# A modulation vector summed on VectorE between the steps of a recurrence instead of in the scan stages, with earlier loads put off, four tiles at once on TensorE, and a reordered tail

## The chip, the cores and the metric

One core of a Trainium2 chip runs one kernel: a whole transformer-like layer in float32. The metric is the device time of one execution in microseconds (us), the median of the runs of one kernel. The core has a matrix engine (TensorE, "PE" in the profile, its weight loads "PEld"), VectorE ("DVE"), ScalarE ("ACT"), GpSimd ("POOL") and SyncE ("SP"), which here only issues DMAs. SP, ACT and POOL each have a DMA queue of their own; all share 16 DMA engines.

## The reference, cut to what matters

The layer has a modulation (adaLN), a mixer with two branches, and a PEER feed-forward with 512 expert rows for each of the 256 tokens.

```python
mod_l = split(silu(c) @ w_ada + b_ada, 6)             # 2048 x 12288: six vectors of 2048
n = modulate(rmsnorm(h), mod[0], mod[1])              # for the 256 tokens x and the 256 of ctx
z = n @ w_in                                          # 2048 x 7168
ya = s5_mixer(z[:, :1024])                            # state-space scan, 64 groups of 16 channels
yb = lru_mixer(z[:, 1024:2048]) * gelu(z[:, 2048:3072])   # conv, gates, gated linear recurrence
m = sigmoid(z[:, 3072:5120]) * (ya @ w_proj_a) + sigmoid(z[:, 5120:]) * (yb @ w_proj_b)
h = x + mod[2] * (m @ w_out)
f = modulate(rmsnorm(h), mod[3], mod[4])
q = f @ w_query; top 16 of 16384 experts for each token and head (8 heads)
out = rmsnorm(h + mod[5] * sum_k g_k * gelu(f . u[e_k]) * v[e_k])    # rows of 2048 gathered
```

Modulation vector 3 (`LATE_CHUNKS[1]`, the shift of the second norm) is the one that moves here: silu(c) times 16 row blocks of 128 x 2048 of `w_ada`, 1 MB each.

## The kernel before, in words

The program is a queue written out by hand for each engine, with semaphores between them. Weights come in units of 1 MB through a ring of five slots (`w_ring`). A planner (`plan`) writes the list `units` with slot and freeing semaphore; SP issues the loads in that order, and each waits until its slot is free (`load_unit`), so that a load that waits holds up all behind it.

1. Front (0 to 173 us). x and ctx are transposed; for g = 0 to 7 four units of `w_ada` are multiplied for two blocks of the first two vectors (`group_unit`, L1223), ScalarE moves them (`group_rows`), VectorE scales nT, and `front_product` (L1248) adds this part of the first six columns of z. The weights of `front_product` are `w6[g]`, 768 KB each, loaded from ACT's queue four groups ahead (`load_w6`); POOL loads the S5 matrices (`cnat`, 1 MB) after three units are used. `output_weights` transposes them in g = 1 and 2.
2. Recurrence (173 to 348 us). Ten more columns of z, 512 wide (`columns`, L1261), nearly one for each k = 0 to 7 of the recurrence: TensorE gates(k), ScalarE `gates`, `roots`, VectorE `conv`, `q_of`, `scans` (rt, ig and ag have three buffers). Sixteen units of vector 2 (`late_unit`, L1204) are multiplied on TensorE, two in a row in the middle of each column, through slots 3 and 4. ScalarE does in order for each column: evacuate it, gates(k), roots(k-1). POOL stores u (`u_dram`) for each k and waits for it.
3. `lag_zero` (L1276, 256 small matmul records) with the weights Bb that VectorE has just made (L1049 to L1054), then eight G columns, 256 wide.
4. Sixteen scan stages. In each: TensorE does two columns of z for the gates (32 records each), the matmuls of `s5_params` (L1372, L1382), `s5_states` (L1395), `s5_out` (L1410, L1412). ScalarE evacuates; POOL does `imaginary_product`, `rotations`, two stores and `build_pb`; VectorE does `state_scan`, `build_m` and `last_vector` (L1134): one unit of vector 3, in three pieces. Each stage loads three units: two of w_in, one of w_ada.
5. `last_rows(1)` sums vector 3 over the partitions, then projections with w_glu, w_pa, w_pb (to 893 us) and w_out (to 1007 us), with vectors 4 and 5 on VectorE.
6. PEER (from 1009 us): 256 gathers of u rows and 256 of v rows, 1 MB each, from POOL's queue, v four behind u (`LAG`); VectorE does the dots (L1881), in groups of two (`GROUP`) ScalarE the gelu and the diagonal weights, TensorE adds the v rows (L2016). The weights of a group are made after the dots of the next group. At the end the final norm.

Of the kernel before, what the change touches and what calls it, by code (L numbers as in the profile page):

```python
# [9 lines left out]
ALU = mybir.AluOpType  # L10
# [3 lines left out]
P = 128  # L14
# [23 lines left out]
LATE_PER_PAIR = {3: 0, 4: 4, 5: 4, 6: 4, 7: 4}  # L38
# [15 lines left out]
def build(nc, t):  # L54

    ctx = ExitStack()
    with ctx:
# [90 lines left out]
        for n, count in LATE_PER_PAIR.items():  # L148
            plan_first(n + 1, turn[(2 * n + 2) % 3])
            plan_late(count)  # L150
            plan_second(n + 1, turn[(2 * n + 3) % 3])
        last_wide = n + 1
# [6 lines left out]
        last_at = []  # L159
# [52 lines left out]
        def unit(pe, u):  # L212
# [6 lines left out]
              (ada_at, last_at, pair_at, glu_at, fin_at, fin_count), acc_full, acc_free, unit_done, ada_used,  # L219
# [33 lines left out]
def mixer(nc, t, ctx, sem, w_ring, ident, mT, nT, scol, notfirst, units, load_unit, unit, places, acc_full, acc_free,  # L253
          unit_done, ada_used, late_sems, fin_full, fin_used, mods_dram, u_dram, y_dram, gates_dram):

    ada_at, last_at, pair_at, glu_at, fin_at, fin_count = places
    last_used, last_sum, mod_free, mods_out, vec_in = late_sems
    with ExitStack() as st:  # L258
# [19 lines left out]
        last_c = sb("last_c", [P, 256])  # L278
# [28 lines left out]
        def take(n):  # L307
# [15 lines left out]
        kst = take(GS * NLAG * H).rearrange("p (g n h) -> p g n h", g=GS, n=NLAG)  # L323
# [12 lines left out]
        sums = [(zu.rearrange("p b s c -> p (b s c)"), 0, 1024), (big[:, 13888:14656], 1024, 1792),  # L336
                (last_c[:, :], 1792, 2048)]
# [21 lines left out]
        id0, id_ready = sem("id0"), sem("id_ready")  # L359
# [10 lines left out]
        bb_ready, kz_full, kz_done = sem("bb_ready"), sem("kz_full"), sem("kz_done")  # L370
        gst_out, sgate_in = [sem("gst_out0"), sem("gst_out1")], [sem("sgate_in0"), sem("sgate_in1")]
# [39 lines left out]
        def toeplitz(sp, s):  # L411

            sp.wait_ge(k_copied, 3 * s + 3)
# [8 lines left out]
        def _(sp):  # L422
# [14 lines left out]
            for u in range(RING, NUNITS_HERE + RING):  # L437
                s, x = divmod(u - STAGE_UNITS, 3)
# [5 lines left out]
        def _(pool):  # L444
            link = stepper(pool, pool_s)

            pool.memset(ident[:], 0.0).then_inc(id0, 1)
            pool.wait_ge(id0, 1)
# [10 lines left out]
            pool.wait_ge(ada_used, 3)  # L459
# [16 lines left out]

            pool.wait_ge(acc_free, V0 + NB)
# [13 lines left out]

            for k in range(KW):
                pool.wait_ge(acc_free, U0 + k + 1)
# [110 lines left out]
        def _(act):  # L604
# [39 lines left out]
            for g in range(NG8):  # L644
# [5 lines left out]
                if g == 0:  # L650
# [1394 lines left out]
```

## Time and profile before

| | |
|---|---|
| median of 3 runs | 2380.9 us (2379.0 to 2382.27) |
| the profiled execution | 2378.94 us; span from first to last instruction 2377.1 us |
| busy | PE 2025.9 us (85%), DVE 1393.9 (59%), POOL 1041.7 (44%), ACT 457.7 (19%) |
| front | 0 to 172.8 us |
| recurrence | 172.8 to 348.05 us |
| lag_zero | 348.05 to 360.37 us |
| G columns and first column of stage 0 | 360.37 to 424.82 us |
| scan stages, from one L1372 to the last L1418 | 424.82 to 737.37 us |
| projections | 737.37 to 1007 us |
| PEER | 1009 to 2377.1 us |

The span is what one execution shows; some 2 us of the measured time lie around it. In a row of the timeline the first number is the start, the second the time to the end of the last of its instructions, and the bracket is the idle time of that engine ahead of it with what ended it. A float32 matmul is two records (x32 is 16 matmuls).

### The profile page before, as it was taken

To read this page: it belongs to the slowest core of one execution; us is meant where nothing else is said; L and a number is where in the kernel's file an instruction comes from. 1 tells how busy PE (TensorE), PEld (TensorE's weight loads), DVE (VectorE), ACT (ScalarE), POOL (GpSimd) and SP (SyncE) were. 2 spreads that over 40 slices of the span, in tenths; PEclk is the share of its full clock that TensorE was granted. 3 is DMA by queue.
4 is the path that set the end of the run, shared out by engine and by line. 5 is a ranking of instruction groups with operands and counts; after the bars stand their busy time and mean duration, and the time that the engine had idled before them with its cause. 6 is when DMAs were issued, how large, how long until landed. Compare 5 with 4: busy or idle time off the path is not lost.

```text
span 2377.1 us, 21789 instructions
## 1 busy us (share of the span) xinstructions
PE 2025.9 (85%) x8106; PEld 1176.7 (50%) x8106; DVE 1393.9 (59%) x2142; ACT 457.7 (19%) x977; POOL 1041.7 (44%) x883
## 2 busy tenths in 40 slices
PE   5999999999999999989789888777777777777776
PEld 3443348887887878875344444222322222222222
DVE  4643651799995533546555664565566566655644
ACT  3116740233331000121011111101110111111011
POOL 1001005799993100035455555555555455555552
PEclk8999999999999999999999999999999999999999
DMA  9965558565657898879999999999999999999996
GB/s 335 305 195 146 208 179 159 182 192 172 200 188 237 302 335 303 294 274 411 413 414 418 421 421 422 421 422 421 421 421 422 422 421 422 421 422 422 421 422 255
DMA packets 253017, 789.33 MB, mean 332 GB/s; under 512 B 25160, under 2 KB 170768, under 8 KB 177520
## 3 DMA queue, kind: packets, MB, share of 16 engines
q0 software_dynamic: 80528, 558.18, 58.0%
q1 hardware_dynamic: 160704, 220.31, 28.0%
q10 hardware_dynamic: 11680, 9.44, 1.3%
q8 instruction: 65, 1.06, 0.2%
q14 instruction: 40, 0.33, 0.0%
HBM read 774.20 MB, written 9.47 MB: 330 GB/s over the span
## 4 chain that ended last, share of the span: by engine, by line
DMA 39%; PE 20%; issue 1%; POOL 1%; DVE 0%; ACT 0%; DVEq 0%; ACTq 0%; POOLq 0%
DMA vb<-in_peer_v,eidx 39%; PE ps L2016 11%; PE ps L1917 4%; PE ps L1972 3%; PE ps L1949 1%; POOL vb L1613 0%; DMA w_ring<-in_w_out 0%; PE ps L1936 0%; POOL nT L1613 0%; DVE h L1855 0%; DVE f L1854 0%; PE ps L1987 0%; DVE h L1862 0%; ACT L1688 0%; ACT L1719 0%
## 5 line engine op out<-in xcount | busy, mean ns | idle before, releaser
L2016 PE MATMUL ps<-vb,diag 128*128 128x512 f32 x2048 | 954.1, 613 | 274.0 <-DMA vb<-in_peer_v,eidx 269.7
L2016 PEld LDWEIGHTS ps<-vb,diag 128*128 128x128 f32 x2048 | 378.5, 193 | 839.9 <-DMA vb<-in_peer_v,eidx 439.3
L1613 POOL DMA_INDIRECT vb<-in_peer_v,eidx x256 | 422.3, 1650 | 547.7 <-PE ps L2016 536.7
L1881 DVE CUSTOM_DVE_ANT_0 nT<-nT,f 128x2048 f32<-128x2048 f32 x170 | 389.3, 2292 | 340.1 <-DMA nT<-in_peer_u,eidx 339.4
L1261 PE MATMUL ps<-nT,w_ring 128*128 128x256 f32 (+1 forms) x1600 | 427.5, 426 | 0.3 <-issue 0.3
L1261 PEld LDWEIGHTS ps<-nT,w_ring 128*128 128x128 f32 x1600 | 303.0, 192 | 114.8 <-issue 82.3
L1881 DVE CUSTOM_DVE_ANT_0 mT<-mT,f 128x2048 f32<-128x2048 f32 x86 | 197.0, 2291 | 188.2 <-DMA mT<-in_peer_u,eidx 188.0
L1719 ACT ACTIVATE gel<-hd 128x2 f32<-128x2 f32 x128 | 26.0, 204 | 1118.2 <-DVE hd L1881 1118.2
L1613 POOL DMA_INDIRECT nT<-in_peer_u,eidx x170 | 174.2, 1025 | 51.8 <-issue 51.8
L1917 PE MATMUL ps<-w_ring,mT 128*128 128x256 f32 x512 | 111.5, 380 | 4.4 <-PEq L258 2.3
L1613 POOL DMA_INDIRECT mT<-in_peer_u,eidx x86 | 88.4, 1028 | 47.0 <-issue 25.9
L1917 PEld LDWEIGHTS ps<-w_ring,mT 128*128 128x128 f32 x512 | 96.9, 190 | 19.1 <-issue 6.1
L1972 PE MATMUL ps<-fT,w_ring 128*128 128x256 f32 x448 | 98.9, 379 | 0.6 <-ACT scol L1647 0.6
L1972 PEld LDWEIGHTS ps<-fT,w_ring 128*128 128x128 f32 x448 | 84.9, 190 | 16.4 <-issue 5.5
L1446 PE MATMUL ps<-big,w_ring 128*128 128x256 f32 x384 | 85.5, 384 | 5.0 <-DMA w_ring<-in_w_proj_a 3.5
L1703 ACT ACTIVATE diag<-ident,wgt 128x128 f32<-128x128 f32 x256 | 88.5, 393 | 2.2 <-DVE wgt L1839 0.3
L1446 PEld LDWEIGHTS ps<-big,w_ring 128*128 128x128 f32 x384 | 73.7, 193 | 17.1 <-issue 4.8
L1248 PE MATMUL ps<-nT,big 128*128 128x512 f32 x144 | 67.8, 606 | 2.6 <-ACT nT L648 2.6
L494 POOL DMA_DIRECT2D u_dram<-zu x8 | 4.4, 547 | 144.7 <-ACT zu L715 144.7
L1604 POOL DMA_DIRECT2D mods_dram<-diag x1 | 0.6, 600 | 121.1 <-DVE diag L1867 121.1
L470 POOL DMA_DIRECT2D mT<-in_lru_w_r x4 | 2.7, 687 | 116.0 <-PE ps L1223 116.0
L594 POOL DMA_DIRECT2D big<-gates_dram x16 | 11.4, 717 | 93.2 <-DVE mT L1176 93.2
(367 smaller groups left out, 2108.1 us busy)
## 6 DMA issues: line engine op xcount, KB each, us to landing
w_ring<-in_w_ada SPq DMA_DIRECT2D x96, 1024.0 KB, 7.0
w_ring<-in_w_in SPq DMA_DIRECT2D x50, 1024.0 KB, 5.3
w_ring<-in_w_out SPq DMA_DIRECT2D x16, 1024.0 KB, 7.4
w_ring<-in_peer_w_query SPq DMA_DIRECT2D x16, 1024.0 KB, 25.5
w_ring<-in_w_proj_b SPq DMA_DIRECT2D x8, 1024.0 KB, 7.9
w_ring<-in_w_proj_a SPq DMA_DIRECT2D x8, 1024.0 KB, 7.8
big<-in_w_in ACTq DMA_DIRECT2D x6, 768.0 KB, 7.9
big<-big SPq DMA_DIRECT2D x128, 32.0 KB, 3.5
```

The costliest lines, as they stand in the source:

```text
L594: pool.dma_start(sgate[:, c % 2, x].rearrange("p (k n) -> p k n", k=2), gates_dram[x * KD + 2 * c:x * KD + 2 * c + 2].rearrange("k p n -> ...
L1248: last = pe.matmul(ps[:, acc_bank(b), :], w6[g][:, kb, b * P:(b + 1) * P], nT[:, k, :], start=(k == 0), stop=(k == KD - 1))
L1261: last = pe.matmul(ps[:, (a + j) % 2, 0:hi - lo], w[k // UK][:, k % UK, j * P:(j + 1) * P], nT[:, k, lo:hi], start=(k == 0), stop=(k == KD ...
L1446: last = pe.matmul(ps[:, bank, j * T:(j + 1) * T], w[:, k, j * P:(j + 1) * P], y[:, k], start=(k == 0), stop=(k == KW - 1))
L1613: pool.indirect_dma_start(ring[m % n], None, table, bass.IndirectOffsetOnAxis(ap=eidx[:, i % 3, j:j + 1], axis=0))\
L1703: act.activation(diag[:, m % NDIAG], ident[:], ACT.Copy, scale=wgt[:, i % 2, m % K:m % K + 1])\
L1719: act.activation(gel[:, i % 2, lo:lo + GROUP], hd[:, i % 2, lo:lo + GROUP], ACT.Gelu_apprx_tanh)\
L1881: v.tensor_tensor_reduce(ub[m % n_u], ub[m % n_u], f[:, i // HEADS], 1.0, 0.0, ALU.mult, ALU.add, hd[:, i % 2, m % K:m % K + 1]).then_inc( ...
L1917: last = pe.matmul(ps[:, 4 * (c % 2) + i, 0:COLS], mT[:, k, i * P:(i + 1) * P], w[k // UK][:, k % UK, :], start=(k == 0), stop=(k == KD - 1))
L1949: last = pe.matmul(ps[:, 4 + i, j * P:(j + 1) * P], w[k // UK][:, k % UK, j * P:(j + 1) * P], fT[:, k, i * P:(i + 1) * P], start=(k == 0), ...
L1972: last = pe.matmul(ps[:, 4 + c % 2, j * T:(j + 1) * T], w[k // UK][:, k % UK, j * P:(j + 1) * P], fT[:, k, :], start=(k == 0), stop=(k == ...
L2016: last = pe.matmul(ps[:, 4 * tile + c, :], diag[:, m % NDIAG], vb[m % NV][:, c * 512:(c + 1) * 512], start=(r == 0), stop=(r == HEADS * K ...
```

## The change

- Vector 3 leaves the scan stages. `load_row` on POOL's queue brings its 16 blocks one by one into slot 4, each only after the block ahead of it is used (`last_used`); `row_vector` on VectorE adds them up (704 + 1344 columns): block 0 after the first four convs, block 2k+1 between `q_of(k)` and `scans(k)`, block 2k+2 between `scans(k)` and the next conv. POOL's loads stand ahead of the stores of u in its queue. `last_rows(1)` comes ahead of the scan stages, into bank 7. A stage then loads two units, not three.
- Vector 2's units go through slot 3 alone, one at the middle and one at the end of a column's half instead of two at the middle.
- `load_w6(g + 2)` after group g+1's rows, where it was `load_w6(g + 4)`; `cnat` waits for nine units, not three; `output_weights` in g = 3 and 4.
- VectorE makes Bb in the G columns (`input_weights` after k = 2 and 3), and `lag_zero` comes after the G columns.
- The kernel matmuls of `s5_params` (L1372) put group g's result at partition 32 g, all four groups of one r after another; ScalarE evacuates them with four activations of 16 x 224 where it had two of 16 x 448 (`k_copied` 5 for each stage, not 3).
- PEER: the last two groups of two become four of one, v rows close up from four to one behind u over the last six rows, and ScalarE does a square root on a dummy ahead of both norms.

```diff
-LATE_PER_PAIR = {3: 0, 4: 4, 5: 4, 6: 4, 7: 4}
+LATE_PER_PAIR = {3: (1, 0), 4: (3, 1), 5: (3, 1), 6: (3, 1), 7: (3, 0)}
...
-                ada_at.append(plan_ada(*late[n_late[0]], 3 + n_late[0] % 2))
+                ada_at.append(plan_ada(*late[n_late[0]], 3))
...
+        row_free = freed_by[4]
+        freed_by[4] = (last_used, KD)
...
-            if n >= len(pairs) - NSTAGE:
-                plan_last()
...
-        sums = [(zu.rearrange("p b s c -> p (b s c)"), 0, 1024), (big[:, 13888:14656], 1024, 1792),
-                (last_c[:, :], 1792, 2048)]
+        sums = [(last_c[:, :], 0, 704), (big[:, 13312:14656], 704, 2048)]
...
-            pool.wait_ge(ada_used, 3)
+            pool.wait_ge(ada_used, 9)
...
+            def load_row(k):
+                if k == 0:
+                    pool.wait_ge(row_free[0], row_free[1])
+                else:
+                    pool.wait_ge(last_used, k)
+                at = LATE_CHUNKS[1] * D
+                pool.dma_start(row_view(w_ring[:, 4]), t["w_ada"][0, k * P:(k + 1) * P, at:at + D])\
+                    .then_inc(row_in, 16)
+            load_row(0)
...
+            load_row(1)
             for k in range(KW):
+                for n in (2 * k + 2, 2 * k + 3):
+                    if n < KD:
+                        load_row(n)
                 pool.wait_ge(acc_free, U0 + k + 1)
                 pool.dma_start(u_dram[k], zu[:, k % 2]).then_inc(u_out, 16)
                 pool.wait_ge(u_out, 16 * (k + 1))
...
-                    load_w6(2)
-                    load_w6(3)
-                if g + 4 == NG8 - 1:
-                    act.wait_ge(s5_setup, 8)
-                if g + 4 < NG8:
-                    load_w6(g + 4)
...
+                if g + 2 < NG8:
+                    load_w6(g + 2)
...
-                for x in range(2):
-                    act.activation(kst[0:H, :, Q * x:Q * x + Q - 1, :],
-                                   ps[0:H, 2 + x, 0:GS * (Q - 1) * H].rearrange("p (g n h) -> p g n h", g=GS, h=H),
+                lags = kst.rearrange("p g (x n) h -> p g x (n h)", x=2)
+                for g in range(GS):
+                    act.activation(lags[0:H, g, :, 0:(Q - 1) * H], ps[32 * g:32 * g + H, 2:4, 0:(Q - 1) * H],
                                    ACT.Copy).then_inc(k_copied, 1)
...
             for k in range(4):
                 conv(k)
+            row_vector(0)
             for k in range(KW):
                 q_of(k)
+                row_vector(2 * k + 1)
                 scans(k)
+                if k < KW - 1:
+                    row_vector(2 * k + 2)
                 if k + 4 < KW:
                     conv(k + 4)
...
-                if s < NSTAGE:
-                    last_vector(s)
...
-                spots = ((), ()) if c < KW // 2 else ((7, 7), (7, 7))
+                spots = ((), ()) if c < KW // 2 else ((7, 15), (7, 15))
...
-            lag_zero()
             for c in range(KW // 2):
                 for _ in columns(G0 + 2 * c, T, 2 * T):
                     pass
+            lag_zero()
+            last_rows(1)
...
-                for g in range(GS):
-                    for r in range(2):
+                for r in range(2):
+                    for g in range(GS):
                         for x, part in ((1, slice(0, N)), (0, slice(N, P))):
-                            last = pe.matmul(ps[0:H, 2 + x, g * nk:(g + 1) * nk], Bb[part, r, s * GS + g, :],
+                            last = pe.matmul(ps[32 * g:32 * g + H, 2 + x, 0:nk], Bb[part, r, s * GS + g, :],
...
+    groups = [range(m, m + GROUP) for m in range(0, NI * K - 2 * GROUP, GROUP)]
+    groups += [range(m, m + 1) for m in range(NI * K - 2 * GROUP, NI * K)]
+    rows_behind = {m: LAG - 1 - (m - (NI * K - 3 * GROUP)) // GROUP for m in range(NI * K - 3 * GROUP, NI * K)}
...
+            act.activation(root_in, ident[:, 0:1], ACT.Sqrt)
             last_squares()
```

## Rows read from the trace of the kernel before

**Rows 1.** The page's chain that ended last, shares of the span by engine.
```profile
DMA 39%; PE 20%; issue 1%; POOL 1%; DVE 0%; ACT 0%; DVEq 0%; ACTq 0%; POOLq 0%
```

**Rows 2.** Windows: start:end, length, busy of five engines, PE clock, DMA share, GB/s.
```profile
0.00:45.00 45.00, 26.66 (x194) 17.38 (x194) 20.87 (x70) 18.15 (x28) 7.25 (x15) 0.92 1.01 324
...
172.80:348.05 175.25, 171.95 (x514) 67.86 (x512) 93.35 (x135) 111.62 (x154) 11.49 (x13) 1.00 0.50 167
348.05:360.37 12.32, 6.97 (x257) 6.75 (x256) 5.67 (x6) 1.88 (x2) 4.34 (x8) 0.85 0.96 293
...
424.82:737.37 312.55, 304.80 (x2265) 263.96 (x2265) 291.89 (x286) 106.93 (x198) 278.94 (x254) 0.99 0.61 187
644.68:725.05 80.37, 77.55 (x581) 67.00 (x581) 78.03 (x77) 28.53 (x52) 74.88 (x69) 1.00 0.61 190
```

**Rows 3.** Timeline of PE in the front.
```profile
41.52 3.70 PE L1248 MATMUL ps<-nT,mT 128*128 128x512 f32 x8
...
55.15 1.93 PE L1223 MATMUL ps<-w_ring,scol 128*32 128x256 f32 x16 [8.05 <-DMA w_ring<-in_w_ada]
57.01 5.04 PE L1248 MATMUL ps<-nT,mT 128*128 128x512 f32 x8
```

**Rows 4.** Timeline of PE: a late unit, and the start of lag_zero.
```profile
213.47 1.07 PE L1204 MATMUL ps<-w_ring,scol 128*32 128x512 f32 x8 [0.57 <-DMA w_ring<-in_w_ada]
...
351.32 6.28 PE L1276 MATMUL ps<-Cc,Bb 128*16 128x16 f32 x236 [3.19 <-DVE Bb L1054]
```

**Rows 5.** Timelines of ACT and DVE: roots(1), the first instruction of scans(1) and of scans(5).
```profile
234.36 1.15 ACT L698 ACTIVATE big<-big 128x512 f32<-128x512 f32 x2
...
235.61 0.69 DVE L1029 TENSOR_TENSOR big<-big 128x512 f32<-128x512 f32 x1 [6.42 <-ACT big L698]
...
309.93 0.69 DVE L1029 TENSOR_TENSOR big<-big 128x512 f32<-128x512 f32 x1 [10.35 <-ACT big L698]
```

**Rows 6.** DMA issues from 200 to 345 us: count, KB each, median us to landing.
```profile
w_ring<-in_w_ada SPq DMA_DIRECT2D x16, 1024.0 KB, 7.8
w_ring<-in_w_in SPq DMA_DIRECT2D x8, 1024.0 KB, 5.1
u_dram<-zu POOLq DMA_DIRECT2D x7, 256.0 KB, 4.0
```

**Rows 7.** Line L599, three POOL loads of 1 MB at 824 to 845 us.
```profile
DMA to landing us min/median/max: 7.9/10.7/11.8
```

**Rows 8.** Groups by form: count, busy us, mean ns of one, idle before.
```profile
L248 DVE SCALAR_TENSOR_TENSOR big<-w_ring,scol,big 128x2048 f32<-128x2048 f32 x15 | 35.2, 2344 | 0.3
...
L1134 DVE SCALAR_TENSOR_TENSOR zu<-w_ring,scol,zu 128x1024 f32<-128x1024 f32 x15 | 25.7, 1711 | 0.5
...
L1134 DVE SCALAR_TENSOR_TENSOR big<-w_ring,scol,big 128x768 f32<-128x768 f32 x15 | 20.2, 1347 | 0.5
...
L1134 DVE SCALAR_TENSOR_TENSOR last_c<-w_ring,scol,last_c 128x256 f32<-128x256 f32 x15 | 12.1, 806 | 0.5
```

**Rows 9.** Timeline of PE from one stage to the next.
```profile
606.03 1.71 PE L1372 MATMUL ps<-big,Bb 64*16 64x112 f32 x32
...
608.60 7.07 PE L1261 MATMUL ps<-nT,w_ring 128*128 128x256 f32 x32
...
615.85 0.62 PE L1412 MATMUL ps<-big 128*32 128x128 f32 x16
...
625.35 1.71 PE L1372 MATMUL ps<-big,Bb 64*16 64x112 f32 x32
```

**Rows 10.** The window of POOL's first round of stage work.
```profile
388.59:404.57 15.98, 15.68 (x73) 13.52 (x72) 4.12 (x4) 1.13 (x3) 14.94 (x17) 1.00 0.74 237
```

**Rows 11.** Timeline of the end: the last dot, the last v rows, the root.
```profile
2346.12 2.29 DVE L1881 CUSTOM_DVE_ANT_0 nT<-nT,f 128x2048 f32<-128x2048 f32 x1 [2.63 <-DMA nT<-in_peer_u,eidx]
...
2348.61 17.43 PE L2016 MATMUL ps<-vb,diag 128*128 128x512 f32 x40 [1.21 <-DMA vb<-in_peer_v,eidx]
...
2369.67 1.28 ACT L1688 ACT_TABLE_LOAD   x1
```

More of the change, by code:

```diff
@@ L1059, in late_rows, with lag_zero @@
+            def lag_zero():
+                step(tt(kzero[:], ident[0:H, 0:H].unsqueeze(1).to_broadcast([H, G, H]),
+                        dT[:].unsqueeze(2).to_broadcast([H, G, H]), ALU.mult))
+                for b in range(2):
+                    v.wait_ge(kz_full, b + 1)
+                    kz = kzero[:, b * 32:(b + 1) * 32, :].rearrange("p g h -> p (g h)")
+                    tt(kz, kz, ps[0:H, 4 + b, :], ALU.add).then_inc(kz_done, 1)
+                v.wait_ge(kz_done, 2)
             def late_rows(q):
@@ L1269, in columns, with last_rows @@
                     yield
+            def last_rows(q):
+                pe.wait_ge(last_used, KD * q)
+                if q == 2:
+                    pe.wait_ge(acc_free, L0 + KW)
+                for j in range(4):
+                    at = slice(j * 512, (j + 1) * 512)
+                    for total, lo, hi in (sums if q == 1 else [(fin_sum, 0, D)]):
+                        a, b = max(lo, at.start), min(hi, at.stop)
+                        if a < b:
+                            last = pe.matmul(ps[32 * j:32 * j + 32, (7, 0)[q - 1], a - at.start:b - at.start],
+                                             notfirst[:, 1:33], total[:, a - lo:b - lo], start=True, stop=True)
+                last.then_inc(last_sum, 1)
             def lag_zero():
@@ L1359, in _ @@
                     pass
+            lag_zero()
+            last_rows(1)
             def s5_params(s):
@@ L1469, in _ @@
                         fin(c, 1)
-                    last_rows(1)
                 if s < NSTAGE:
@@ L1616, in _ @@
             tu, tv = t["peer_u"][0], t["peer_v"][0]
-            for m in range(NI * K + LAG):
-                if m < NI * K:
-                    if m % K == 0:
-                        pool.wait_ge(idx_ready, m // K + 1)
-                    gather(m, tu, ub, u_in, u_used)
-                if m >= LAG:
-                    gather(m - LAG, tv, vb, v_in, v_used)
+            n_v = 0
+            for m in range(NI * K):
+                if m % K == 0:
+                    pool.wait_ge(idx_ready, m // K + 1)
+                gather(m, tu, ub, u_in, u_used)
+                while n_v <= m - rows_behind.get(m, LAG):
+                    gather(n_v, tv, vb, v_in, v_used)
+                    n_v += 1
+            for m in range(n_v, NI * K):
+                gather(m, tv, vb, v_in, v_used)
         @block.scalar
         def _(act):
+            act.activation(root_in, ident[:, 0:1], ACT.Sqrt)
             for c in range(NCH):
@@ L1877, in _ @@
                     v.wait_ge(gel_done, (i - 1) * (K // GROUP))
-                for m in range(GROUP * g, GROUP * (g + 1)):
+                for m in groups[g]:
                     n_u = len(ub)
```

151 lines of the change are left out of this document (71 added, 80 removed).

## The prediction

> **What bounds the kernel now.** I read the chain that ended last first: 39% of it is DMA of v rows and 20% TensorE [rows 1]. PEER is one DMA stream from 1070 us to the end, and the change leaves its 512 gathers alone. What comes before it shifts it as a whole, so a microsecond on TensorE before 1007 us is a microsecond of the kernel, as long as PEER's own start and end are counted apart.
>
> Then I cut the time before PEER into windows. In the recurrence TensorE works 171.95 of 175.25 us, around lag_zero 6.97 of 12.32, in the scan stages 304.80 of 312.55 [rows 2]. So TensorE is the bound nearly everywhere, and the reader should look for two things: waits between its instructions (the timeline of PE), and work of its own that gets shorter. But the scan stages are close to a second bound: VectorE is busy 291.89 us there and GpSimd 278.94 [rows 2]. From 644.68 to 725.05 us are four stages of 20.1 us, while a stage in which TensorE never waits takes 625.35 - 606.03 = 19.32 us [rows 2, 9]. VectorE and GpSimd stretch each other: a piece of 256 columns of `last_vector` takes 0.81 us and one of 1024 takes 1.71, where 2048 alone take 2.34 [rows 8].
>
> **Part by part.** *Front.* TensorE waits 8.05 us for a unit of w_ada, and its next eight records take 5.04 us where the same eight took 3.70 before the wait [rows 3]: 8.05 + 1.34 = 9.4 us. What is late is bytes: the queues bring 324 GB/s with the DMA engines full, 14.6 MB by 45 us [rows 2]. The unit waited for is the eighth. With x and ctx (4.2 MB), eight units (8.4) and two w6 (1.6), it needs 14.2 MB; three more w6 and cnat (3.4 MB) are in the same stream today and leave it. So it would be there at about 45 us, and TensorE comes for it at 46. I take all 9.4 us. Bounds: 6, if the stream, which then still owes cnat and one w6 per group, falls behind once more, and 10.3, if the group's own matmuls (1.93 us, also slow) get their speed back as well. That the later loads of w6 cost nothing rests on their cover: each has more than the time of one group to land.
>
> *Recurrence, TensorE's side.* The 16 late units stay. Four waits like the 0.57 us one [rows 4] make 3.3 us, being all that TensorE waits here (175.25 - 171.95) [rows 2]. With slot 3 alone, a unit needed at the end of a column can only be asked for when the one at the middle is used, some 7 us earlier (16 records, each twice as long as the 221 ns of the narrow columns [rows 9]), and a unit lands in 5.1 us when alone and 7.8 when others are in the queue [rows 6]. Eight such places with 0 to 1.1 us each: 0 to 8.8 instead of 3.3. I take no change, range -3.3 to +5.5.
>
> *Recurrence, VectorE's side.* This is where the change adds a wait. A column lasts (309.93 - 235.61) / 4 = 18.6 us, and VectorE waits 6.42 of them in front of `scans(1)`, 10.35 when no conv is left to do [rows 5]. Two blocks at 2.34 and a gap cost 4.9 us per k [rows 8]; this fits. But slot 4 is one buffer: block n+1 is asked for when block n is used, so a k cannot take less than 2 x 2.45 + 2L, L being the time from the use of a block to the landing of the next; scans, conv and q_of (12 us in two parts) lie beside the two loads. Behind the waiting block stand scans(k), the next conv and q_of, on which ScalarE's `roots` waits, and behind that its evacuation of the next column, for which TensorE waits two columns on. The last chance is column 15: its evacuation is needed when the first G column is done, 348.05 + 7.1 = 355.1 us. From scans(1) at 235.6: five turns of 4.9 + 2L to scans(6), then L + 2.45 for block 14, 2.5 for q_of(7), for which two passes over 1024 columns cost about one over 2048 [rows 8], 1.2 for the two roots [rows 5] and half of that for the evacuation, as wide as one root. 266.9 + 11 L = 355.1 gives L = 8.0. Up to there nothing shows; every microsecond above costs 11. No row shows such a load. From below: 256 KB from POOL's queue land in 4.0 us [rows 6], the other 0.79 MB take 2.3 us at the 324 GB/s of rows 2: 6.3. From above: 1 MB loads of POOL took 7.9 to 11.8 us, but with the DMA engines full [rows 7]. Here they are half full at 167 GB/s; 16.8 MB more make it 263 [rows 2]. So I take the lower end and 0.9 us of sharing, L = 7.2, cost 0.
>
> Beside it stands the Trainium skill, DMA: Bandwidth & Descriptors, Anatomy of one DMA: a GpSimd DMA takes 2.0 us + bytes / 436 GB/s by its fit, an estimate of 4.4 us for this load when alone, and L near that would make the cost 0 as well. The trace has no lone 1 MB load of POOL's queue to set beside the fit.
>
> *lag_zero.* TensorE waits 3.19 us for Bb in front of it, and of its 12.32 us it works 6.97 [rows 2, 4]. After the change Bb is made in the G columns, where VectorE has two short operations per column, and six more in two of the eight columns fit beside them. The 3.19 us go; of the other 2.2 idle us I credit 0.8. Sum 4.0, bounds 0 and 5.3. `last_rows(1)` leaves the end of the stages and comes in here at the same price: 0.
>
> *Scan stages.* Two effects. TensorE's own: L1372 takes 1.71 us for 32 records, today two tiles at a time [rows 9]; afterwards eight tiles are addressed in turn. L1412, four tiles with 128 columns, needs 0.62 us for 16 records [rows 9], 39 ns each; lag_zero's small ones need 27 ns each (6.28 us for 236) [rows 4]. 32 records make 1.24 or 0.85 us; the streams themselves would allow 0.43. I take 0.9, since 112 columns over eight tiles hide below the issue: 0.8 us less, 18.5 us a stage. The other: VectorE loses 1.71 + 1.35 + 0.81 = 3.9 us a stage [rows 8], so the stages of 20.1 us go. 16 x 18.5 = 296 for 312.55: 16.5 us. Bounds: 3.4 if the tiles give nothing (16 x 19.32 = 309.1) and 23.9 if they run freely (288.6). ScalarE's evacuation grows from two to four activations; it is busy 106.93 of the 312.55 us [rows 2] and hides them. SP's Toeplitz copies stand ahead of other units now, but two units a stage leave them early.
>
> A rule sets a floor under the tiles: by the Trainium skill, TensorEngine Tiling (Array Packing), Instruction Overhead, each matmul costs some 60 cycles whatever its size, an estimate of 25 ns at 2.4 GHz and of 0.8 us for 32 records. The 27 ns of lag_zero's records [rows 4] agree with it, and by it the free run to 288.6 us would be out of reach.
>
> *PEER.* The last u row lands at 2346.12, a v row at 2348.61, so a row takes 2.49 us; the four v rows still out are in at 2358.6, but TensorE works five rows at 3.49 until 2366.0 [rows 11]. Afterwards the order ends u255, v254, v255: u255 lands at 2353.6, its dot and weights are ready near 2357, and only two rows (7.0 us) are left: 2.5 us less. A table load of 1.28 us stands in front of the last root [rows 11], half of it beside VectorE's three small steps: 0.7 us, and much the same at the head of PEER: 1.3. Together 3.8, bounds 1 and 5.
>
> Sum: 9.4 + 0 + 4.0 + 16.5 + 3.8 = 33.7. Against the profiled execution: span 2377.1 - 33.7 = 2343.4, time 2378.9 - 33.7 = 2345.2. That execution is 2 us under the median; 2380.9 - 33.7 = 2347.2.
>
> **The rivals.** (1) *The blocks land late.* L of 9.5 instead of 7.2 costs 16.5 us in the recurrence: 2364. For it: the loads share the engines with late units in bursts; against it: the mean share stays below three quarters. Chance 0.13.
> (2) *The same, slower than before.* From L = 8.0 + 33.7 / 11 = 11.1 on the whole gain is gone. At the 11.8 us of rows 7 TensorE waits 42 us at the end of the recurrence: 2389. It needs engines as full as there; the window's 167 GB/s speak against it. Chance 0.05.
> (3) *The tiles do nothing* (one after another, or a switch between tile shapes that costs as much): stages of 19.32 us, 309.1, time 2360. Against it: L1412's 39 ns. Chance 0.10.
> (4) *GpSimd becomes the stages' bound.* Its first round, with VectorE busy for 1.13 us only, lasts 15.98 us with one small DMA issue in it [rows 10]; with a second and larger one some 16.8; in the late stages 20.1. VectorE's busy time falls by a fifth, so the 3.3 us of stretch by as much: 19.4 us a round. It starts with about 10 us in hand and would use up 14: 4 us more, 2351; without that reserve 14 more, 2361. Beside it stands the Trainium skill, GPSIMD Engine Reference, Specifications: GpSimd shares its SBUF interfaces with VectorE. Chance 0.10.
>
> **How the numbers follow.** The forecast has 0.62: 2347, its own range 2337 to 2356. The best bounds of all parts give 2336; the rivals that are still gains lie at 2351 to 2364. I give 2337 to 2367, which leaves out rival 2, a part of rival 1 and the far good end. A measurement of this kernel tells 0.2% (4.8 us) from no change. Faster: forecast, rivals 3 and 4 and nearly all of 1, 0.93; same 0.02; slower 0.05.
>
> **What would show it.** TensorE's first wait for w_ada near 55 us gone, and the windows' end of the front near 163 us; L1276 with no wait on Bb; L1372 at 0.9 us with its 32 records; stages of 18.5 us with VectorE idle 3 to 4 us in each; L2016's last unbroken run shorter than five rows. Wrong would be: VectorE waiting for w_ada by way of POOL's queue with the idle time in front of scans gone, and then TensorE waiting in front of a G column for ScalarE; or GpSimd without a pause and TensorE waiting in front of L1382 or L1410.

## The result, and the profile after

The changed kernel takes 2344.85 us in the median of 4 executions (2331.79 to 2350.51), the kernel before 2379.95 (4 executions): a ratio of 0.9844, 95% interval 0.9807 to 0.988. Forecast were 2347, range 2337 to 2367. The total is right, but two of its terms are not, and they cancel. The four executions also lie 19 us apart, where those of the kernel before lie within 4.4 us; the profiled one is the fastest (time 2331.79, span 2329.7). A second profile of the same kernel (`after_again` below, span 2340.8) is nearer the median, and each stretch is read in both.

| stretch, us | before | after | after again | change | forecast |
|---|---|---|---|---|---|
| front, to the first column | 173.18 | 162.17 | 163.02 | -11.0, -10.2 | -9.4 |
| recurrence, to the end of its last column or late unit | 174.87 | 172.81 | 173.74 | -2.1, -1.1 | 0 |
| G columns, lag_zero, column 1 of stage 0 | 76.77 | 73.16 | 81.34 | -3.6, +4.6 | -4.0 |
| stages, 15 periods | 300.23 | 272.05 | 272.05 | -28.2, -28.2 | -16.5 |
| last stage to the first v row | 344.04 | 343.28 | 344.91 | -0.8, +0.9 | 0 and head of PEER |
| first v row to the end | 1308.0 | 1306.2 | 1305.7 | -1.8, -2.3 | -3.8 with the head |

The windows of the profile after, which answer to [rows 2] (start:end, length, busy us of PE, PEld, DVE, ACT, POOL, PE clock, DMA share, GB/s), for the first 45 us, the recurrence, the stages, and four stages of them:

```profile
0.00:45.00 45.00, 26.70 (x194) 17.44 (x194) 20.86 (x70) 18.15 (x28) 3.72 (x11) 0.92 1.01 338
161.85:334.98 173.13, 172.51 (x514) 67.31 (x512) 125.42 (x158) 112.57 (x156) 20.00 (x28) 1.00 0.77 253
408.14:691.40 283.26, 283.26 (x2265) 243.31 (x2264) 225.02 (x237) 113.91 (x230) 259.20 (x254) 1.00 0.51 147
571.00:643.83 72.83, 72.83 (x589) 62.44 (x594) 59.39 (x65) 30.28 (x60) 67.33 (x66) 1.00 0.52 151
```

In the stages TensorE never waits any more: 283.26 us busy in 283.26. VectorE is idle (72.83 - 59.39) / 4 = 3.4 us in each. GpSimd has 67.33 busy us in the four, so it pauses for 1.4 us in each, and TensorE never waits for it.

The timeline of PE after, at the places of [rows 3], [rows 4] and [rows 9]:

```profile
45.18 1.93 PE L1245 MATMUL ps<-w_ring,scol 128*32 128x256 f32 x32
47.05 3.70 PE L1270 MATMUL ps<-nT,mT 128*128 128x512 f32 x8
...
336.32 41.68 PE L1283 MATMUL ps<-nT,w_ring 128*128 128x256 f32 x192 [1.34 <-issue]
379.69 14.05 PE L1283 MATMUL ps<-nT,w_ring 128*128 128x256 f32 x64 [1.69 <-issue]
393.67 6.54 PE L1313 MATMUL ps<-Cc,Bb 128*16 128x16 f32 x255
...
570.95 0.60 PE L1410 MATMUL ps<-big,Bb 64*16 64x112 f32 x32
571.48 1.09 PE L1420 MATMUL ps<-ident,big 128*128 128x128 f32 x8
...
589.16 0.60 PE L1410 MATMUL ps<-big,Bb 64*16 64x112 f32 x32
```

The wait of 8.05 us for w_ada is gone, the eight records behind it take 3.70 us again, lag_zero starts with no wait for Bb. L1410 (L1372 of before) ends its 32 records so early that the next line starts 571.48 - 570.95 = 0.53 us after it, and a stage takes 589.16 - 570.95 = 18.21 us. New are two waits of TensorE in the G columns, for nothing that the profile names. In `after_again` the second is 6.17 us:

```profile
338.76 27.86 PE L1283 MATMUL ps<-nT,w_ring 128*128 128x256 f32 x128 [2.00 <-issue]
372.80 30.89 PE L1283 MATMUL ps<-nT,w_ring 128*128 128x256 f32 x128 [6.17 <-issue]
```

The four columns behind it take 30.89 us where the four ahead took 27.86: from 369 to 379 us the granted clock is 0.50, the lower of the two levels (1.2 and 2.4 GHz). TensorE had stood since 366.6, and it worked from 372.80 on for 6 us at that clock. In the changed kernel's first profile the clock there is 1.00. The window of `after_again`:

```profile
369.00:379.00 10.00, 6.20 (x15) 4.99 (x16) 2.71 (x3) 0.00 (x0) 2.96 (x4) 0.50 1.09 231
```

The DMA side of it is the time from issue to landing of the w_in units that SP issues from 345 to 372 us, first in the profile after, then in `after_again`:

```profile
L211 SPq DMA_DIRECT2D w_ring<-in_w_in x4: 368/368/4436, 347.0 to 364.2; - x4
...
DMA to landing us min/median/max: 16.2/18.6/26.2
```

```profile
L211 SPq DMA_DIRECT2D w_ring<-in_w_in x4: 367/368/6922, 349.4 to 366.7; - x4
...
DMA to landing us min/median/max: 16.8/20.3/24.7
```

The unit issued at 349.4 in `after_again` lands 23.3 us later, at 372.7, and TensorE goes on at 372.80. The wait ahead of the first G column ends in the same way: its unit lands at 336.2 and 338.7 us in the two profiles, and TensorE starts at 336.32 and 338.76. What runs beside the units of the second wait are POOL's 32 loads of U (the copy of u that the scan stages read back from memory), 64 KB each; from 348 to 372 us the DMA engines are full and move 125 to 174 GB/s (in stretches of 6 us). The first row is the kernel before, the second the profile after:

```profile
356.57 17.77 POOL L499 DMA_DIRECT2D nT<-u_dram  x32 [6.73 <-DMA u_dram<-zu]
342.78 17.78 POOL L514 DMA_DIRECT2D nT<-u_dram  x32 [7.06 <-DMA u_dram<-zu]
```

The kernel before has the same slow loads. Its w_in units of 372.6 and 376.0 us take 17.4 and 17.0 us, and TensorE waits for the first of them, which lands at 390.0:

```profile
L210 SPq DMA_DIRECT2D w_ring<-in_w_in x2: 367/368/368, 372.6 to 376.0; - x2
...
DMA to landing us min/median/max: 17.0/17.2/17.4
...
390.12 34.77 PE L1261 MATMUL ps<-nT,w_ring 128*128 128x256 f32 x160 [0.30 <-issue]
```

By this trace lag_zero is why it waits for 0.30 us only: while TensorE waited for Bb and did lag_zero (348 to 360 us), three units asked for at 348.2 to 349.2 could land (by 364.4), so that four units, enough for four columns, were there or nearly so when the G columns began at 360.37.

The blocks of vector 3 (L484, 16 loads by POOL), first how long VectorE waits for them (22.3 us in 8 waits), then their time from issue to landing:

```profile
  DVE last_c L1058: 22.3, 8
...
DMA to landing us min/median/max: 5.2/5.7/10.7
```

And the tail, which answers to [rows 11]: the last u dot, the last two v rows, the table load now beside them, the root.

```profile
2309.15 2.29 DVE L1916 CUSTOM_DVE_ANT_0 nT<-nT,f 128x2048 f32<-128x2048 f32 x1 [4.96 <-DMA nT<-in_peer_u,eidx]
...
2312.16 7.10 PE L2051 MATMUL ps<-vb,diag 128*128 128x512 f32 x16 [0.77 <-ACT diag L1735]
2312.39 1.28 ACT L1761 ACT_TABLE_LOAD   x1
...
2323.49 0.20 ACT L1720 ACTIVATE rss<-rss 128x1 f32<-128x1 f32 x1 [0.61 <-DVE rss L1894]
```

### The profile page after: what moved, and what is told of

Its sections match the earlier page's. It is cut to its first block, busy times and chain, and to the rows that moved or that the text cites. A ratio compares the mean times of both kernels' runs of the same rounds, so it can differ in the third digit from the quotient of the medians.

```text
span 2329.7 us, 21810 instructions
## 1 busy us (share of the span) xinstructions
PE 1998.1 (86%) x8106; PEld 1152.6 (49%) x8106; DVE 1368.2 (59%) x2128; ACT 465.4 (20%) x1013; POOL 1031.9 (44%) x899
## 4 chain that ended last, share of the span: by engine, by line
DMA 39%; PE 21%; issue 1%; POOL 1%; DVE 1%; ACT 0%; DVEq 0%; POOLq 0%
DMA vb<-in_peer_v,eidx 37%; PE ps L2051 12%; PE ps L1952 5%; PE ps L2007 4%; DMA nT<-in_peer_u,eidx 2%; POOL vb L1641 1%; PE ps L1984 1%; DMA w_ring<-in_w_out 0%; PE ps L1971 0%; DVE nT L1916 0%; PE ps L2022 0%; POOL nT L1641 0%; DVE h L1890 0%; DVE f L1889 0%; DVE h L1897 0%
## 5 line engine op out<-in xcount | busy, mean ns | idle before, releaser
L1752 ACT ACTIVATE gel<-hd 128x2 f32<-128x2 f32 (+1 forms) x130 | 26.3, 203 | 1125.8 <-DVE hd L1916 1125.7
L1486 PEld LDWEIGHTS ps<-big,w_ring 128*128 128x128 f32 x384 | 73.8, 193 | 16.8 <-issue 4.1
L1130 DVE TENSOR_TENSOR big<-big 128x512 f32<-128x512 f32 x32 | 37.4, 1169 | 53.7 <-ACT big L763 53.1
L484 POOL DMA_DIRECT2D w_ring<-in_w_ada x16 | 8.5, 534 | 122.9 <-DVE big L1058 122.9
```

What stands on the lines that cost most here:

```text
L1130: ins = tt(x, Ssb, rot[:, s % 2, r:r + 1].to_broadcast([P, 2, GS, NC]), ALU.mult)
L1486: last = pe.matmul(ps[:, bank, j * T:(j + 1) * T], w[:, k, j * P:(j + 1) * P], y[:, k], start=(k == 0), stop=(k == KW - 1))
L1752: act.activation(gel[:, i % 2, lo:hi], hd[:, i % 2, lo:hi], ACT.Gelu_apprx_tanh)\
```

## The experiments

**The changed kernel again** (`after_again`), no edit.

> The changed kernel once more, unchanged, since its four executions lay between 2331.8 and 2350.5 us where the kernel before stays within 4.4 us. Theory 1 (the clock): an execution near 2345 has stretches before PEER in which TensorE's granted clock is lower than in the profiled one, and the waits are the same; its span is then some 12 us longer in those stretches alone. Theory 2 (the loads): the same clock, but waits of TensorE for w_ada, of VectorE for rows or of PEER for u and v that the profiled execution does not have. Expected time 2345, range 2332 to 2351.

2341.17 us (2335.12 to 2343.86), ratio 0.9823 (0.9804 to 0.9842). Theory 2 in the main: of the 11.1 us between the two profiles, 0.9 lie in the front, 1.6 in the recurrence with the wait behind it, 7.5 from the first G column to stage 0 (4.5 of longer waiting and 3.0 of columns at the lower clock behind it), none in the 15 periods, 1.6 behind them, and -0.5 in PEER. All eight executions of the changed kernel together have a median of 2342.2.

**The tiles taken back** (`no_tiles`).

```diff
-                for r in range(2):
-                    for g in range(GS):
+                for g in range(GS):
+                    for r in range(2):
...
-                            last = pe.matmul(ps[32 * g:32 * g + H, 2 + x, 0:nk], Bb[part, r, s * GS + g, :],
+                            last = pe.matmul(ps[0:H, 2 + x, g * nk:(g + 1) * nk], Bb[part, r, s * GS + g, :],
```

> The changed kernel with the tiles of the s5_params kernel matmuls and their evacuation as before (one column tile, two activations, k_copied 3 a stage). Theory 1 (TensorE bounds the stages once vector 3 has left them, and the tiles are worth what their line shows): the line's 32 records take 1.71 us again instead of 0.60, a stage 18.2 + 1.1 = 19.3 us, 15.6 stages 17 us, so 2345 + 17 = 2362. Theory 2 (the tiles were only filling idle time and the relief of VectorE gave the stages their gain): a stage stays near 18.2, time 2345 to 2348.

2361.23 us (2358.27 to 2370.24). Two neighbouring stages in its timeline of PE:

```profile
437.11 1.71 PE L1410 MATMUL ps<-big,Bb 64*16 64x112 f32 x32
...
456.43 0.75 PE L1410 MATMUL ps<-big,Bb 64*16 64x112 f32 x12
```

456.43 - 437.11 = 19.32 us a stage, with no wait: theory 1. (The second row is cut by the window.) Without vector 3 TensorE alone bounds the stages, and the 1.11 us of the line are 1.11 us of the stage.

**Only the order taken back** (`tiles_g_outer`): the two loops as in the diff above, the four places kept.

> The changed kernel with the same four column tiles, but the loop over groups outside the loop over re and im, as before the change: four records in a row go to one column tile, two to each row half. Theory 1 (what matters is that neighbouring matmuls lie in different column tiles): the line goes back towards 1.7 us, a stage to 19.3, time 2362. Theory 2 (the placement alone does it): 0.6 us, 18.2 us a stage, time 2345. Something between, some 1.1 us, would mean that both row halves and the column tiles share in it: 2353.

2342.03 us (2338.19 to 2348.68), the line at 0.64 us, a stage 18.25 us. The expectation of theory 1 fell: it is not the turn but the place. Why 32 records at one partition range take 1.71 us and at four 0.64 in either order is not settled.

**The tiles alone on the kernel before** (`tiles_alone`): vector 3 stays in the stages.

> The kernel before with the tiles and the four activations alone; vector 3 stays in the stages. Theory 1 (VectorE with vector 3 holds the stages at 20.0 us, TensorE is no longer their bound): TensorE's line is 1.1 us shorter and its waits 1.1 us longer, stages 19.7 to 20.0, time 2375 to 2380. Theory 2 (TensorE alone bounds the stages and the effects add up): 15.6 x 1.1 = 17 us less, 2363.

2373.69 us (2372.66 to 2379.35), ratio 0.9975 (0.996 to 0.9989). Four stages and the first row of two of them:

```profile
590.34:670.70 80.36, 73.12 (x580) 62.57 (x581) 78.02 (x77) 30.31 (x60) 75.01 (x69) 1.00 0.62 191
```

```profile
590.34 0.43 PE L1410 MATMUL ps<-big,nT 128*32 128x128 f32 x8 [1.81 <-issue]
...
610.43 0.43 PE L1410 MATMUL ps<-big,nT 128*32 128x128 f32 x8 [1.82 <-issue]
```

VectorE is busy 78.02 of 80.36 us and the stage takes 20.09 us, to the hundredth what four stages of before took [rows 2]; TensorE's gain has become a wait of 1.8 us. The 15 periods together got shorter by 4.7 us. In the mean of the last 14 periods, 20.14 us before, the tiles alone save 0.25 us, vector 3's leaving alone 0.82, both together 1.93.

The mean hides how the periods of the kernel before differ: nine take 19.3 us (the first of them 18.3), four 20.1, one 21.15 and one 25.89. In the last TensorE waits, for nothing that the profile names, and then works at a granted clock of 0.61 (573.6 to 580.4 us), so that 32 records take 9.30 us and not 7.07:

```profile
573.64 0.42 PE L1410 MATMUL ps<-big,nT 128*32 128x128 f32 x8 [3.17 <-issue]
...
577.48 9.30 PE L1261 MATMUL ps<-nT,w_ring 128*128 128x256 f32 x32
```

So the 28.2 us of the 15 periods are 16.7 of the shorter line (15 x 1.11), 8.4 of these two long periods and 3.1 of the four at 20.1. `no_tiles`, without vector 3, has no long period; `tiles_alone`, with it, has two (24.19 and 23.4 us).

**lag_zero where it was** (`lag_zero_early`), and **in the middle of the G columns** (`lag_zero_middle`).

```diff
+            lag_zero()
             for c in range(KW // 2):
                 for _ in columns(G0 + 2 * c, T, 2 * T):
                     pass
-            lag_zero()
```

In `lag_zero_early` VectorE's making of Bb is also ahead of the G columns again; the cut shows TensorE's side.

> The changed kernel with Bb and lag_zero again ahead of the G columns, as before the change. In the changed kernel TensorE waits inside the G columns for w_in, 1.7 us in one execution and 6 to 9 us in others, while POOL's 32 small-packet loads of U hold the DMA engines. Theory 1 (those waits come from the move of lag_zero, which had given the loads 12 us more): the waits in the G columns vanish, the 3.2 us wait for Bb and the slow clock behind it return, TensorE comes to stage 0 within 2 us of where it does now, executions lie closer together, time 2340 to 2344. Theory 2 (the move gained its 4.0 us and the waits come from elsewhere, such as slot 4 being held to the end of the recurrence): waits in the G columns stay and 4 us are added, time 2346 to 2349.

2348.0 us (2345.51 to 2348.28), ratio 0.9866 (0.985 to 0.9883): slower than the changed kernel by 6. Its PE timeline:

```profile
348.52 6.33 PE L1313 MATMUL ps<-Cc,Bb 128*16 128x16 f32 x236 [11.75 <-DVE Bb L1088]
357.16 0.72 PE L1313 MATMUL ps<-Cc,Bb 128*16 128x16 f32 x20 [2.31 <-issue]
357.81 57.99 PE L1283 MATMUL ps<-nT,w_ring 128*128 128x256 f32 x256
```

The first half of theory 1 holds: all eight G columns run through without a wait. The second does not: the wait for Bb is 11.75 us and not 3.2, since VectorE leaves the recurrence later, with the last block still to add: it ends its last scans 4.3 us behind TensorE's columns (341.03 and 336.77 us), where it was 4.3 us ahead of them in the kernel before.

> The changed kernel with Bb made after the first two G columns and lag_zero after the fourth, so that TensorE has 7 us of work that needs no load at the place where it waits for w_in. Theory 1 (the loads are late by 1.7 to 9 us behind the loads of U): most of the waits goes and no wait for Bb comes, 3 to 6 us less than the changed kernel in its usual executions, time 2337 to 2340. Theory 2 (TensorE waits there for something else, or the late load moves on to the next pair with its whole lateness): time as the changed kernel, 2341 to 2345.

2337.77 us (2334.8 to 2340.82), ratio 0.9819 (0.9801 to 0.9836). Inconclusive for the theories: the columns have no wait in their middle, but lag_zero itself has one of 5.31 us between record 235 and the last 21, with no releaser named, and the way from the first G column to stage 0 is as long as in `after_again` (79.45 us and 79.34). Where the 4 us in its median come from, this profile doesn't show.

**Vector 3 left out** (`rows_away`: only block 0 is loaded and summed), and **each block late** (`rows_twice`, `rows_half_more`). The cut is that of the last two; N is 2048 and 1024.

```diff
+                if k > 0:
+                    pool.dma_start(row_view(w_ring[:, 4])[:, 0:N], t["w_ada"][0, k * P:(k + 1) * P, at:at + N])\
+                        .then_inc(row_in, 16)
+                    pool.wait_ge(row_in, 32 * k)
                 pool.dma_start(row_view(w_ring[:, 4]), t["w_ada"][0, k * P:(k + 1) * P, at:at + D])\
```

> The changed kernel without the loads and sums of blocks 1 to 15 of vector 3 (only block 0 is summed, so the vector is left incomplete). It shows what vector 3 costs in its new place. Theory 1 (it is hidden there): front and stages as they are; only the late units' waits (1 to 3 us) and the 2 us in front of the first G column go, 2339 to 2342 with the loads of U left. Theory 2 (late rows set the end of the recurrence, the slot the first w_in loads of the G columns): the waits in the G columns go as well, time 2330 to 2335.

2336.49 us (2330.53 to 2337.73). The waits for late units and the one ahead of the first G column are gone, the one in the middle is not (4.03 us; w_in lands in 16.5 to 28.5 us). By the medians vector 3 costs some 6 us in its new place (2342.2 against 2336.5), and the time lies between the two theories. The profiles show 2.0 and 3.6 us of it: from the first column to the first G column it is 172.1 us here, 174.2 and 175.7 in the two profiles of the changed kernel. The rest lies within what the wait in the middle differs by from execution to execution. The mechanism is theory 1's: vector 3 is not what makes w_in late beside the loads of U.

> The changed kernel with each block of vector 3 but the first loaded twice in a row, the second after the first has landed, so that the time L from a block's use to the next one's landing goes from 5.7 to some 11 us. Theory 1 (my sum: nothing shows up to L = 8.0 us, and 11 us for each one above): the recurrence's end, or the wait in front of the G columns, is (11 - 8.0) x 11 = 33 us later, time 2377, range 2366 to 2388. Theory 2 (VectorE's slack is larger, since scans, conv and q_of lie beside the loads in ways that the sum left out): under 15 us, 2345 to 2358. Theory 3 (the engines are already short of bytes there): TensorE waits for late units and w_in too and more than 45 us are lost.

> The changed kernel with half a block of vector 3 loaded ahead of each whole block but the first, and waited for, so that L, the time from a block's use to the landing of the next, is some 9.5 us (5.7 without the half, 12.2 in the mean where the whole block was loaded twice, which cost 79 us). Theory 1 (my sum on record: 11 us for each us above 8.0): 16 us over the changed kernel, 2358. Theory 2 (the chain runs through all 14 turns up to block 14, each L + 2.6 us, from 201 us to the 339.5 us at which ScalarE must have q_of(7): threshold 7.3 us, 14 us for each us above): 31 us, 2373, and a little more for the slower clock behind each wait, up to 2380.

`rows_twice` takes 2420.23 us (2418.09 to 2422.27), `rows_half_more` 2399.73 (2397.07 to 2402.22): slower than the kernel before (ratios 1.0172 and 1.0089). VectorE's line of sums in `rows_half_more`, and TensorE's waits, first there and then in `rows_twice`:

```profile
L1062 DVE SCALAR_TENSOR_TENSOR last_c<-w_ring,scol,last_c x15: 950/952/953, 206.0 to 402.5; 128x704 f32<-128x704 f32 x15
...
  DMA w_ring<-in_w_ada: 99.5, 15
```

```profile
371.33 10.03 PE L1287 MATMUL ps<-nT,w_ring 128*128 128x256 f32 x32 [10.31 <-ACT zu L730]
396.98 36.80 PE L1287 MATMUL ps<-nT,w_ring 128*128 128x256 f32 x160 [15.62 <-ACT zu L730]
443.72 16.58 PE L1287 MATMUL ps<-nT,w_ring 128*128 128x256 f32 x64 [9.94 <-issue]
```

```profile
391.62 9.12 PE L1287 MATMUL ps<-nT,w_ring 128*128 128x256 f32 x32 [17.89 <-ACT zu L730]
419.31 22.75 PE L1287 MATMUL ps<-nT,w_ring 128*128 128x256 f32 x96 [18.58 <-ACT zu L730]
```

The place is the one that the prediction named as the last chance: ScalarE's evacuation of column 15, behind the roots, behind the block. From block 1 to block 14 a turn takes 14.2 us in the one and 15.9 in the other, less 2.65 of work: L is 11.5 and 13.2 us, more than the 9.5 and 11 that I expected, for the loads also meet late units. Block 14 is begun at 390.1 and 412.5 us and used up at 392.7 and 415.1; TensorE goes on 4.3 us after that in both. Thirteen turns lie between block 1 and block 14, so each us of L costs 13 us there, 14 with the load of block 1 itself; the sum on record had 11. The two times differ by 20.5 us for 1.7 us of L.

The threshold follows from the same chain. In the profile after, TensorE is due at that place at 343.2 us, so block 14 must be used up by 338.9. Block 1 is begun at 198.7 us there (at 206.0 in the two runs, whose first load is late as well). (338.9 - 198.7 - 2.6) / 13 = 10.6 us a turn, less 2.65: L = 7.9 us, an estimate. The sum on record had 8.0; theory 2 of `rows_half_more`, with 7.3, counted fourteen turns from block 1's end at 201 us, where there are thirteen.

**w6 four groups ahead again** (`front_w6_ahead`).

```diff
-                if g + 2 < NG8:
-                    load_w6(g + 2)
+                if g == 0:
+                    load_w6(2)
+                    load_w6(3)
+                if g + 4 < NG8 - 1:
+                    load_w6(g + 4)
+                if g == NG8 - 3:
+                    load_w6(NG8 - 1)
```

> The changed kernel with w6 loaded four groups ahead again (w6[7] after group 5), while the S5 matrices stay late. Theory 1 (the three w6, 2.4 MB of the 3.4 that left the stream ahead of the eighth unit, are the larger part): TensorE waits again for w_ada near 55 us, 8.05 x 2.4 / 3.4 = 5.7 us and the slow records behind it, time 2341 + 6 = 2347. Theory 2 (the S5 matrices, with their small packets, are what delayed the unit): no wait or one under 2 us, time 2341 to 2343.

2345.51 us (2342.78 to 2351.16), between the theories, and its interval (0.9845 to 0.9885) overlaps that of the changed kernel. Its only wait for w_ada above half a microsecond:

```profile
75.51 1.07 PE L1250 MATMUL ps<-w_ring,scol 128*32 128x256 f32 x16 [1.58 <-DMA w_ring<-in_w_ada]
```

This does not tell the theories apart, for the three w6 did not go out where they did before. There they stand ahead of group 1's rows and go out at 40.4 to 41.4 us, with the eighth unit (issued at 31.5) on its way; here they stand behind these rows and go out at 48.0 to 49.1, when the eighth unit has landed (at 43.8). First the kernel before, with the seventh and the eighth unit, then this run with the eighth:

```profile
L612 ACTq DMA_DIRECT2D big<-in_w_in x3: 374/480/494, 40.4 to 41.4; - x3
...
L210 SPq DMA_DIRECT2D w_ring<-in_w_ada x2: 881/1340/1800, 30.6 to 31.5; - x2
...
DMA to landing us min/median/max: 15.4/19.5/23.6
```

```profile
L627 ACTq DMA_DIRECT2D big<-in_w_in x3: 458/481/488, 48.0 to 49.1; - x3
...
L211 SPq DMA_DIRECT2D w_ring<-in_w_ada x1: 878/878/878, 32.2 to 32.2; - x1
...
DMA to landing us min/median/max: 11.7/11.7/11.7
```

What the run shows is that w6 issued at 48 us costs later units 1.6 us of wait. Which part of the 3.4 MB made the eighth unit late stays open. The count of bytes needs no such difference: all 17.6 MB at 324 GB/s make 54.3 us, and the unit landed at 55.1 in the kernel before; 14.2 MB make 43.8, and it landed at 44.2 in the profile after.

**The loads of U spread** (`u_loads_paced`) and **in the same queue but not spread** (`u_loads_act_once`).

```diff
                 act.activation(gst[:, k % 2, 0], ps[:, k % 2, 0:T], ACT.Gelu_apprx_tanh).then_inc(acc_free, 1)
+                if k == 0:
+                    act.wait_ge(u_out, 16 * KW)
+                for g in range(GS):
+                    src = u_dram[:, :, k, :].rearrange("k (a b h) c -> b h (k a) c", h=H, b=GS)[g]
+                    act.dma_start(U[k * H:(k + 1) * H, :, g, :], src).then_inc(u_in, 16)
```

POOL's own 32 loads of U are taken out in both runs; the cut is that of `u_loads_paced`.

> The changed kernel with the 32 loads of U taken from POOL's queue, where they go out one behind the other in 18 us, and put into ScalarE's, four behind the evacuation of each G column, so that they are spread over 50 us. Theory 1 (these loads make the w_in loads beside them last 16 to 26 us, for which TensorE waits 1.7 to 9 us in the G columns): w_in lands in 5 to 10 us there, the wait in the middle of the G columns is gone, time 2333 to 2338 and executions closer together. Theory 2 (the rate of small packets is the limit however they are spread): as many us of waits, only in other places, and the last U loads late for stage 0: 2341 to 2350.

2332.54 us, five executions from 2332.36 to 2337.77, ratio 0.9813 (0.9796 to 0.983). Landing of the w_in units from 345 to 372 us, and the G columns:

```profile
L211 SPq DMA_DIRECT2D w_ring<-in_w_in x4: 368/368/372, 348.6 to 365.9; - x4
...
DMA to landing us min/median/max: 5.6/6.8/8.0
```

```profile
337.97 55.49 PE L1283 MATMUL ps<-nT,w_ring 128*128 128x256 f32 x256 [1.65 <-issue]
```

Theory 1: median landing 6.8 us for 18.6 and 20.3, all 256 records of the eight columns without a break, and executions within 5.4 us in place of 19. From the first G column to stage 0 it takes 70.8 us, in `after_again` 79.3, in the fastest execution of the changed kernel 71.8. It beats the kernel before surely, and most likely the changed one: six of that kernel's eight executions lie above its slowest. The size stays loose: 9.7 us by the medians, but 2 to 7 us by the ratios to the kernel before (0.9813 against 0.9823 and 0.9844), and the intervals overlap.

> The changed kernel with the 32 loads of U in ScalarE's queue, but all at once behind the first G column, as POOL issued them, not spread over the eight columns. Theory 1 (it is the spreading that keeps w_in quick): w_in beside them takes 15 us and more again, TensorE waits 2 to 9 us in the G columns, time 2338 to 2346. Theory 2 (it is the queue: POOL's was the slow one for small packets, in its own loads and in those beside it): w_in lands in 5 to 10 us, no wait, time as with the spread loads, 2332 to 2336.

2348.6 us (2345.81 to 2350.77), ratio 0.9859. The test doesn't tell the theories apart, for it brought a wait of its own:

```profile
372.77 27.40 PE L1284 MATMUL ps<-nT,w_ring 128*128 128x256 f32 x116 [10.79 <-ACT gst L778]
```

ScalarE stood for 24.08 us in the issue of its 32 loads and evacuated no column meanwhile. Of two w_in units beside them one took 7.3 us, as with the spread loads, and one 13.7, between those and POOL's. How much of POOL's 16 to 26 us is its queue and how much the burst stays open.

## Why the prediction was right, point by point

- *Front, 9.4 us: right*, 10.2 and 11.0. Wait and slow records are gone as said; the rest is the group's own sixteen records back at speed (0.9 us) and a wait of 0.8 us one unit earlier. The count of bytes puts the unit at 43.8 us, and it landed at 44.2. Whether the S5 matrices weigh more than their bytes no run shows.
- *Recurrence, TensorE's side, 0: right in size.* One to three waits of 0.3 to 0.8 us for late units are left of 3.3 us; 1.1 to 2.1 us came in. A new wait of 1.3 to 2.0 us for w_in stands behind them, ahead of the first G column.
- *Recurrence, VectorE's side, 0: right in mechanism, place and threshold.* L was taken as 7.2 us; the load measures 5.7 in the median and is issued some 0.3 us after the block's use, so L is 6.0, under the threshold of 7.9 (8.0 on record). The price above it is 13 to 14 us for each us of L and not 11, since the sum began at `scans(1)` and left out the loads ahead of it. Leaving the vector out gives 2.0 to 3.6 us back by late units and the start of the G columns. By the Trainium skill, DMA: Bandwidth & Descriptors, Anatomy of one DMA, this load was put at 4.4 us when alone; the fastest of 16 measured 5.2, beside other loads. One slip in the sum from below: 0.79 MB at 324 GB/s are 2.4 us, not 2.3.
- *lag_zero, 4.0 us: the step that failed.* "The 3.19 us go" holds. But lag_zero was also the time in which the w_in units of the G columns landed ahead of the loads of U, and beside these loads a unit takes 16 to 26 us; the prediction moved lag_zero without asking what ran beside it. The execution near the median loses 4.6 us in that stretch, the fastest gains 3.6. `lag_zero_early` (no wait in the G columns) and `u_loads_paced` (units in 5.6 to 8.0 us, no wait in their middle) show it from two sides. Most of the difference between the two profiles (7.5 of 11.1 us) lies here.
- *Scan stages, 16.5 us: mis-sized, 28.2 in the periods and 29.3 in the window, beyond its own bound of 23.9.* Two errors. The window holds 15 periods and a remainder of 12.3 us, not 16 periods: 15 x (20.02 - 18.5) + 0.8 = 23.6 would have been the sum, 7.1 more. And the line takes 0.53 us, not 0.9: 5.5 more. By the Trainium skill, TensorEngine Tiling (Array Packing), Instruction Overhead, each matmul has some 60 cycles of overhead, an estimate of 25 ns; the prediction counted it for each of 32 records, and 0.53 us are 17 ns a record, so it is no floor there. For each of the 16 float32 matmuls it is 33 ns, which the page allows. The two effects are worth more together than apart, as `tiles_alone` and `no_tiles` show.
- *PEER, 3.8 us: 1.8 to 2.3 in the tail*, in the order that was worked out (two rows in the last run), and 0.8 at the head in the first profile (from the last squares at 1009.30 to the first v row 59.8 us, there 59.0). In `after_again` the head is 59.8 as before, and the projections ahead of it take 0.9 us more.
- *The rivals.* Blocks did not land late enough for (1) and (2); made late on purpose they gave what (2) describes, at more than its price. (3) was wrong by 1.1 us a stage. (4) did not come: GpSimd's busy time fell from 18.7 us a stage (74.88 / 4) to 16.8 (67.33 / 4) as VectorE's load fell, and it fits into 18.2. Its working also misread [rows 10]: VectorE is busy for 4.12 us there; the 1.13 are ScalarE's.
- Sum, against `after_again`: 12 us too little in the stages, 9 too much around lag_zero, 2 too much in PEER with what lies ahead of it, 2 too little in front and recurrence together. That the total came within 2 us of the median (5 us of that of all eight executions) is luck: two errors of some ten us cancel. The best bounds of all parts give 2333 with the recurrence's 3.3 us, not 2336.

## What to carry to other kernels

Before a stretch of compute that needs no loads is moved, look at what the DMA queues do beside it: it may be the time in which the loads of the next stretch land, and the wait comes back in another place, here with columns at the lower clock behind it. When two engines bound a loop nearly together, price both edits as one: each alone gave 0.25 and 0.82 us a stage, both 1.93. A burst of small loads did best spread over the columns that ran beside it, in a queue whose engine had time to issue them, four at a time and not thirty-two. And when an experiment puts a load back, look in its trace at the time of issue: in `front_w6_ahead` three loads go out 7.6 us later than in the kernel before, and the unit in question has landed by then.

## What the runs showed of the hardware that I had not expected

- 32 records of 64x112 took 1.71 us with all results at partitions 0 to 15 and 0.60 or 0.64 us with four partition ranges, by the order; the next line starts 0.53 and 0.57 us after it, 17 and 18 ns a record.
- While POOL's 32 loads of 64 KB ran and landed, the DMA engines were full at 125 to 174 GB/s (348 to 372 us) and 1 MB units beside them took 16 to 26 us, in the kernel before 17.0 and 17.4; with the same 2 MB in fours from ScalarE's queue, 5.6 to 8.0.
- 32 issues in one go held ScalarE for 24.08 us; in fours, 1.8 to 3.1 us each time.
- lag_zero pauses between record 234 to 236 and its last 20 or 21 when it runs beside loads or close behind them (0.76, 2.15, 2.31 and 5.31 us in four kernels), and not when it runs behind them (`after_again`). The profile names no releaser; what it waits for is open.
